# Hybrid attention block on one core: head 0's probabilities of steps 34 to 51 moved by SBUF to SBUF DMAs and turned by VectorE instead of by TensorE

## What is computed

```python
def mixer_b(q, k, v, rel_table):
    ...
    logits = jnp.einsum('bcqhd,bckhd->bhcqk', qc.astype(jnp.float32),
                        kb.astype(jnp.float32)) * SCALE
    ...
    logits = logits + bias[:, None]
    ...
    p = jax.nn.softmax(logits, axis=-1)
    out = jnp.einsum('bhcqk,bckhd->bcqhd', p.astype(vb.dtype), vb)
    return out.reshape(b, s, B_W)
```

## Time and profile before

| what | us |
|---|---|
| median of three runs | 1034.33 (1033.67 to 1035.46) |
| span of the profiled execution | 1031.9 |
| median less the span | 2.4 |
| TensorE busy | 1023.0 |
| VectorE busy | 770.9 |
| ScalarE busy | 470.5 |

### The profile page before, as it was taken

One profiled execution on the slowest core, in us unless ns is written; L12 is line 12 of the kernel. 1 busy time (PEld: TensorE's weight loads), 2 busy tenths in 40 slices (PEclk: granted clock), 3 DMA queues, 4 the chain that ended last, 5 costly groups with the idle time before them and its releaser, 6 DMA issues.

```text
span 1031.9 us, 15795 instructions
## 1 busy us (share of the span) xinstructions
PE 1023.0 (99%) x5525; PEld 851.0 (82%) x5525; DVE 770.9 (75%) x1506; ACT 470.5 (46%) x978; POOL 219.7 (21%) x218
## 2 busy tenths in 40 slices
PE   9999999999999999999999999999999999999997
PEld 8899887788778888878888888888888888888886
DVE  4955677867688578888988788786444777778997
ACT  6632355545477567836221221311344445454562
POOL 5200000000000003148675674761100000000000
PEclk9999999999999999999999999999999999999999
DMA  9835442111071474045444434446777733454344
GB/s 202 222 98 136 108 134 77 42 47 37 11 225 43 123 188 159 21 143 212 171 167 155 163 134 152 163 144 225 243 243 242 229 103 92 143 194 142 93 142 164
DMA packets 135071, 147.92 MB, mean 143 GB/s; under 512 B 72248, under 2 KB 85440, under 8 KB 132944
## 3 DMA queue, kind: packets, MB, share of 16 engines
q1 hardware_dynamic: 133920, 146.68, 45.7%
q10 hardware_dynamic: 688, 0.20, 0.1%
q0 software_dynamic: 384, 0.04, 0.0%
HBM read 103.65 MB, written 47.49 MB: 146 GB/s over the span
## 4 chain that ended last, share of the span: by engine, by line
PE 94%; DVE 3%; issue 1%; DMA 1%; ACT 0%; POOL 0%; DVEq 0%; ACTq 0%; POOLq 0%
PE ps L2242 27%; PE ps L2244 27%; PE ps L2243 27%; PE ps L2451 3%; PE ps L2465 3%; PE ps L2432 2%; PE ps L2376 1%; DVE wc_lo L1918 1%; PE ps L2411 1%; PE ps L2584 1%; PE ps L2586 1%; PE ps L2572 1%; DMA up_raw<-in_w_up 1%; DVE b_lo L1907 1%; PE ps L2254 0%
## 5 line engine op out<-in xcount | busy, mean ns | idle before, releaser
L2242 PE MATMUL ps<-b_hi,wc_hi 128*128 128x512 f32 x448 | 174.6, 390 | 0.5 <-DVE wc_lo L1918 0.5
L2243 PE MATMUL ps<-tm_lo,sm_hi 128*128 128x512 f32 (+1 forms) x450 | 174.6, 388 | 0.0
L2244 PE MATMUL ps<-tm_hi,sm_lo 128*128 128x512 f32 (+1 forms) x450 | 174.6, 388 | 0.0
L2242 PE MATMUL ps<-tm_hi,sm_hi 128*128 128x512 f32 (+1 forms) x450 | 174.6, 388 | 0.0
L2244 PE MATMUL ps<-b_hi,wc_lo 128*128 128x512 f32 x448 | 174.3, 389 | 0.0
L2243 PE MATMUL ps<-b_lo,wc_hi 128*128 128x512 f32 x448 | 174.3, 389 | 0.0
L1485 ACT ACTIVATE sm_hi<-sm_raw 128x512 fp32r<-128x512 f32 x112 | 70.7, 631 | 161.8 <-DMA sm_raw<-u_matrices 161.8
L2146 DVE TENSOR_TENSOR sm_lo<-sm_raw,sm_hi 128x512 fp32r<-128x512 f32 x112 | 77.4, 691 | 77.9 <-ACT sm_hi L1485 77.3
L2242 PEld LDWEIGHTS ps<-b_hi,wc_hi 128*128 128x128 f32 x448 | 84.1, 188 | 18.3 <-DVE wc_lo L1918 0.9
L2242 PEld LDWEIGHTS ps<-tm_hi,sm_hi 128*128 128x128 f32 x450 | 84.5, 188 | 17.6
L2244 PEld LDWEIGHTS ps<-tm_hi,sm_lo 128*128 128x128 f32 x450 | 84.5, 188 | 17.4
(11 more groups left out here) (261 smaller groups left out, 2063.2 us busy)
## 6 DMA issues: line engine op xcount, KB each, us to landing
u_matrices<-stage SPq DMA_DIRECT2D x112, 256.0 KB, 2.0
sm_raw<-u_matrices SPq DMA_DIRECT2D x112, 256.0 KB, 2.6
up_raw<-in_w_up SPq DMA_DIRECT2D x16, 1024.0 KB, 5.0
w<-in_w_down SPq DMA_DIRECT2D x64, 256.0 KB, 3.8
w_raw<-in_w_in SPq DMA_DIRECT2D x8, 512.0 KB, 3.5
xr<-in_x SPq DMA_DIRECT2D x8, 512.0 KB, 4.3
x_rows<-xr SPq DMA_DIRECT2D x8, 512.0 KB, 4.1
xf<-x_rows SPq DMA_DIRECT2D x8, 512.0 KB, 3.5
```

Of the source, the lines that this page charges most:

```text
L2242: pe.matmul(out, w_hi_, x_hi_, start=start, stop=False)
L2243: pe.matmul(out, w_hi_, x_lo_, start=False, stop=False)
L2244: return pe.matmul(out, w_lo_, x_hi_, start=False, stop=stop)
```

## The change

For steps 34 to 51 (`TURNED_B`) head 0 goes another way, as it does in part of group A already. Head 1 stays on TensorE.

- VectorE writes head 0's biased scores back to PSUM. ScalarE's exponential reads them there and writes `prob_b` with the columns regrouped by quarters of 32.
- ScalarE does head 0's scaling (`normalize` on ScalarE), VectorE only its reciprocal.
- Four DMAs, SBUF to SBUF, move the quarters to `turn_in` (one buffer for even, one for odd steps), 128 pieces of 128 bytes times the number of key blocks each. SyncE issues two of them, ScalarE the other two right behind its scaling. They wait for the scaling and for VectorE's turn of step n-2.
- VectorE turns the landed 32 x 32 blocks into `probT_b` (`turn_probs`) one step later, behind its last scaling.
- `weigh` reads head 0's turned blocks in pieces of 32 and writes its PSUM columns with a stride of 4.
- Head 1's chunk stays: one chunk copied by ScalarE, and for five blocks a second of one block copied by VectorE. Bank 5 is not used here any more. In a pair, the second step's chunk is turned after three triples of fill instead of two.
- TensorE waits before `scores(n)` for head 0's exponential of n-1. The values lie in another order, `[P, 10, T, 64]`, which makes room for a buffer. SyncE's weight and bias loads stand between its exchanges.

```diff
-    if paired(n) and nk <= 2:
-        return [(0, 2 * nk, nk == 1)]
+    if turned_b(n):
+        return [(nk, nk, True)] if nk < B_KEYS else [(nk, 4, True), (nk + 4, 1, False)]
...
+TURNED_B = range(A_STEPS + 2, LATE - 2)
...
-        v_tok = sb("v_tok", 64, [P, T, VW])
+        v_tok = sb("v_tok", 64, [P, VW // 64, T, 64])
...
+        turn_in = [sb(f"turn_in{n}", at, [P, B_KEYS * P]) for n, at in enumerate((64, 204))]
...
+        def exchange_quarters(eng, n, quarters):
+
+            m = keys_of(n) * 32
+            eng.wait_ge(s_pb, pb0 + turns_until(n + 1))
+            if n < TURNED_B[2]:
+                eng.wait_ge(s_pv, A_STEPS)
+            else:
+                eng.wait_ge(s_tb, tb0 + turns_until(n - 1))
+            for a in quarters:
+                eng.dma_start(turn_in[n % 2][32 * a:32 * a + 32, 0:4 * m].rearrange("j (c m) -> j c m", c=4),
+                              sent_probs(n)[:, a * m:a * m + m]).then_inc(s_pld[n % 2], 16)
...
-            load_fill(6)
-            load_fill(7)
-            sp.wait_ge(s_nm, 10 * T)
-            load_bias(6)
-            load_fill(8)
-            load_fill(9)
-            sp.wait_ge(s_nm, 12 * T)
-            load_bias(7)
+            for n in range(A_STEPS + 1, LATE):
+                exchange_step(n)
+                if n % T == T - 1:
+                    sp.wait_ge(s_nm, 2 * n + 2)
+                    load_bias(n // T + 2)
+                elif n % 4 == 1 and n // 4 - 2 < FILL_TILES:
+                    load_fill(n // 4 - 2)
...
+            def normalize(n):
+
+                at = 2 * (n % 2)
+                act.wait_ge(s_ri, 2 * n + 1)
+                nc.scalar.activation(sent_probs(n), sent_probs(n), ACT.Copy, scale=rinv[0][:, at:at + 1]).then_inc(s_pb, 1)
...
                         for hh in range(2):
                             exp(m, hh)
+                        if turned_b(m):
+                            normalize(m)
+                            exchange_quarters(act, m, (2, 3))
...
+            def turn_probs(n):
+
+                dve.wait_ge(*exchanged(n))
+                dve.wait_ge(s_pv, n - 1)
+                cols = slice(0, keys_of(n) * P)
+                nc.vector.transpose(prob_t(n, 0)[:, cols], turn_in[n % 2][:, cols]).then_inc(s_tb, 1)
...
+                if turned_b(n - 1):
+                    turn_probs(n - 1)
...
+                    if turned_b(n - 1):
+                        pe.wait_ge(s_exp, 2 * n - 1)
...
+                if turned_b(n):
+                    pe.wait_ge(s_tb, tb0 + turns_until(n + 1))
...
+                        out_ = ps[64 * hh:64 * hh + 64, 7, (t % 4) * P:(t % 4) * P + P]
+                        if hh == 0 and turned_b(n):
+                            out_ = out_.rearrange("p (j c) -> p c j", c=4)
...
-                    if m == first + 2 and n % T == 3:
+                    if m == first + 3 and n % T == 3:
                         transposes(n, 0)
-                        transposes(n, 1)
```

More of the change, by code:

```diff
@@ L224, in chunks_until, with chunk_column @@
     return sum(len(chunks_of(m)) for m in range(n))
+def chunk_column(n, c):
+    if not turned_b(n):
+        return 0
+    return P if n % T == 1 else 0
 def chunk_banks():
@@ L233, in chunk_banks @@
                 bank = (6, 4, 5)[(len(banks) + A_STEPS // 2) % 3]
-            else:
-                bank = 6 if n < A_STEPS else 5 if paired(n) and n % T == 1 else (6, 5, 6)[c]
-            banks[n, c] = bank, last.get(bank)
+            elif turned_b(n):
+                bank = 6
+            else:
+                bank = 6 if n < A_STEPS else (6, 5, 6)[c]
+            banks[n, c] = bank, last.get(bank) if chunk_column(n, c) != P else None
             last[bank] = n, c
@@ L499, in chunk_copy @@
             heads = probT_b[:, 2 * (n % 2):2 * (n % 2) + 2]
-            out = ps[:, CHUNK_BANKS[n, c][0], 0:count * P]
+            at = chunk_column(n, c)
+            out = ps[:, CHUNK_BANKS[n, c][0], at:at + count * P]
+            if turned_b(n):
+                return heads[:, 1, first % nk * P:(first % nk + count) * P], out
             if nk == B_KEYS:
@@ L794, in shift_values @@
                     sp.wait_ge(s_tab, 32 * g)
-                sp.dma_start(v_odd[g][0:64], v_tok[64:P, first - 1:end - 1, 0:P]).then_inc(s_tab, 16)
-                sp.dma_start(v_odd[g][64:P], v_tok[0:64, first:end, 0:P]).then_inc(s_tab, 16)
+                sp.dma_start(v_odd[g][0:64], v_tok[64:P, 0:2, first - 1:end - 1]).then_inc(s_tab, 16)
+                sp.dma_start(v_odd[g][64:P], v_tok[0:64, 0:2, first:end]).then_inc(s_tab, 16)
             shift_values(0)
@@ L2409, in weigh_a @@
                         cols = slice(64 * hh, 64 * hh + 64)
+                        values = odd_values(t)[:, hh] if t and half == 0 else v_tok[:, hh, t]
                         out_ = ps[cols, 7, :].rearrange("p (q i n) -> p q i n", q=2, i=2)[:, (r + 1) % 2, :, 64 * half:64 * half + 64]
-                        last = pe.matmul(out_, values[:, cols], probT_a[r % 2][:, heads, 64 * half:64 * half + 64],
+                        last = pe.matmul(out_, values, probT_a[r % 2][:, heads, 64 * half:64 * half + 64],
                                          start=True, stop=True)
@@ L2447, in transposes @@
                     pe.wait_ge(s_pta if chunks_of(former[0])[former[1]][2] else s_ptd, copied(*former))
-                pe.wait_ge(s_p, 2 * n + (start + count - 1) // nk + 1)
+                pe.wait_ge(s_p, probs_made(n, (start + count - 1) // nk))
                 for i in range(count):
                     hh, k = (start + i) // nk, (start + i) % nk
-                    last = pe.transpose(ps[:, bank, i * P:(i + 1) * P], prob_of(n, hh)[:, c0 + k * P:c0 + (k + 1) * P], ident[:])
+                    at = chunk_column(n, c) + i * P
+                    last = pe.transpose(ps[:, bank, at:at + P], prob_of(n, hh)[:, c0 + k * P:c0 + (k + 1) * P], ident[:])
                 last.then_inc(s_pt, 1)
@@ L2518, in _ @@
                 elif not paired(n - 1):
[L2519 to L2520 removed]
+                    for c in range(1 if turned_b(n - 1) else 2):
+                        transposes(n - 1, c)
                 for m in range(first, end):
[L2522 removed]
+                    if m == first + 3 and n % T == 3:
                         transposes(n, 0)
[L2524 to L2526 removed]
+                    elif m == first + 2 and keys_of(n - 1) == B_KEYS:
+                        transposes(n - 1, len(chunks_of(n - 1)) - 1)
                     fill(m)
```

73 lines of the change are left out of this document (54 added, 19 removed).

## The result

The changed kernel takes **1048.95 us** (median of 4 runs, 1048.25 to 1050.34) beside 1034.0 us (1033.42 to 1035.46) before: a ratio of 1.0147, 95% interval 1.0135 to 1.016. It is slower, as forecast, but by 14.95 us where 4.7 were forecast, and outside the range of 1031 to 1046. The profiled execution took 1048.35 us with a span of 1046.5 us, against 1031.9 before: +14.6 us.

The account below looks back on a forecast made before the run. TensorE, busy for 99% of the span, was taken to bound the kernel. The terms -7.0 + 5.9 + 2.0 + 2.9 + 0.9 = +4.7 us on 1034.33 gave 1039.0 us, range 1031 to 1046.

Parts of the forecast that it names:

- the three kinds of idle time: TensorE idle before 43's turn (some 2 us, three times), before products at 37, 45, 53 (0.65), before a fill.
- term A: Steps 34/35, 42/43, 50/51: TensorE waits for ScalarE's chunk copy behind its DMA issues, 1.95 us three times, +5.9 us.
- d: Time of one DMA issue on ScalarE, taken as 0.63 us; it enters the sum 16 times.
- C and D: Steps 45 to 47, 37 to 39 (+2.9 us) and 39/40, 47/48 (+0.9): TensorE waits for VectorE's late fill eviction.
- B: Steps 36/37, 44/45, 52/53: TensorE waits for VectorE's transpose before the products, 0.65 us three times, +2.0 us.
- Saving: Steps 34 to 51: 67 transposes of head 0 leave TensorE at 0.105 us each, -7.0 us.
- Strided write: Head 0's products with the values write PSUM with a stride: taken as 0, at most 7.8 us.
- Landings, SyncE's issues, value layout: Quarters' landing, SyncE's two issues a step and the values' new first-stage layout: costed at nothing.
- ScalarE's exponential from PSUM: ScalarE reads head 0's scores from PSUM instead of SBUF: 0.12 us shorter for 512 columns.
- rival 1: Issues on ScalarE are cheap (0.05 us, or the engine runs on): -7.0 + 3.8 = -3.2, 1031.1 us; chance 0.14.
- Rival 3: Dearer still: strided write at its bound, 1046.8 us, or queues delaying each other's issues, about 1049 us; chance 0.08.

Follow-up runs that it names:

- The two bank experiments: Against the changed kernel: bank 5 for the second chunk of a pair, 1042.11 us; bank 5 for every second chunk, 1041.74 us.
- the first experiment: The changed kernel with all four quarters of every exchange issued by SyncE and none by ScalarE: 1031.21 us.
- the last: The changed kernel with all quarters issued by SyncE, VectorE's transpose ahead of its scaling at some steps, bank 6 for all chunks: 1029.76 us.
- a bank experiment: The changed kernel with bank 5 instead of 6 for the second chunk of a pair (steps 35, 43, 51): 1042.11 us.

## Why the prediction was wrong

Its sign and its mechanism hold: ScalarE's issues stand in its own stream ahead of a copy that TensorE waits for, and taken away they leave a kernel that is faster than before. The signs that it named are there, 173 transposes of prob_b instead of 240 and the three kinds of idle time. Its size fails in one step, the stop of term A, which was sized too short and priced at its length alone. By the account above, +4.7 was to be -7.0 + 5.9 + 2.0 + 2.9 + 0.9, and +14.6 is -4.8 + 9.5 + 5.1 + 1.0 + 3.0 + 0.8.

- **The step that failed: A, +5.9.** It measured 9.5, and the clock behind its stops took 5.1 more. I had taken d = 0.63 from SyncE's row. SyncE's own issues here have a median of 0.599, but ScalarE's take 0.58 and 0.86 where both queues issue in pairs, and the engine starts its next work 0.1 to 0.4 us after that. The stops were 2.90 to 3.41 us instead of 1.95.
- **The omission inside it: the clock, +5.1.** I priced a stop of TensorE at its length. The earlier trace rows showed 1.00 throughout, in a stage where TensorE never stood, and nothing in that row says what happens when it does.
- **C and D, +3.8.** Right in size, at another instruction. VectorE's lateness was to be met at the eviction, 1.45 us twice and 0.45 twice. It was met at the copy just ahead of it, where the bank rule, which I had read only for the pairs, holds TensorE: 1.26, 1.28, 0.22 and 0.22 us, 3.0 in all. The two bank experiments agree: with that wait taken away it returns at the eviction. Places that I had not walked gave 0.8 more.
- **B, +2.0.** 1.0 in the changed kernel in two waits of 0.43 and 0.57 us, 1.8 in three waits of 0.6 where ScalarE issues nothing or one. The size of each wait, 0.65, was right; at step 37 of the changed kernel TensorE came too late to meet it.
- **Saving, -7.0.** TensorE's busy time fell by 4.8 only, in the first experiment (119.9 to 115.1) and by the account above, and by 6.2 in the last (113.7). The price of 0.105 a transpose stands: six of them took 0.63 us to the next fill before (229.92 to 230.55) and three take 0.30 now (235.23 to 235.53). The lower figure is at least in part waits that busy time hides, such as the 0.22 us at each of the three places of B in the first experiment; I have not traced all of it.
- **Strided write, 0.** Right. The products of two steps with five blocks (40 matmuls in the trace) take 2.33 us to the next instruction in the changed kernel (223.55 to 225.88) as they did before, head 0's written with the stride.
- **Landings, SyncE's issues, value layout, 0.** Issue to landing has a median of 2.3 us. VectorE's transpose waits for them 3.0 us in all in the first experiment, which TensorE sees at most in B. With SyncE's issues doubled no new wait of TensorE comes up.
- **ScalarE's exponential from PSUM** was to be 0.12 us shorter; for 640 columns it is 798 ns against 824 from SBUF, 0.03.

The rivals: rival 1's value for issues that cost nothing, 1031.1, is what the kernel without issues on ScalarE takes (1031.21), by -4.8 + 2.3 and not by -7.0 + 3.8; that the two sums end 0.1 us apart is in part luck. Rival 3 named 1049 us, which is the time by luck, and not the cause: no issue of the changed kernel was doubled to 1.26, the longest took 0.894. *The lock between two sequencers that the Trainium skill's "Perfetto Trace Analysis" (DMA Instruction, HWDGE) describes agrees with the direction in which ScalarE's second issue went, from 0.62 us alone to 0.86 beside SyncE's second. It would not tell why the first, made beside SyncE's first, stays at 0.58; that the lock causes the rise no run shows. The ~50 ns of the Trainium skill's "DMA: Bandwidth & Descriptors" (Anatomy of one DMA) for the gpsimd path bears on none of these issues, as the measured 0.55 us minimum shows.*

## What to carry to other kernels

Price a DMA issue on a computing engine as work of that engine, by the row of that very queue under the same company, and give the issues to the queue on which nothing waits behind them. Price a stop of TensorE at its length and look at the granted clock behind it: each fall cost 1.7 us here on top of the stop. It fell behind all three stops of 2.9 us and more in the change, but also behind one of 1.86 us and not behind another of 1.95, so read the clock from the trace and don't infer it from the length. When one wait of a tight chain is removed, look for the same delay at the next place before counting it as a gain.

## What was unexpected of the hardware

ScalarE's issue of the same descriptors (128 pieces, SBUF to SBUF) took a median of 0.580 us when it issued one beside SyncE's three, and 0.624 when it issued four alone. When both issued two, its first took 0.58 and its second 0.86, while SyncE's stayed at 0.60 wherever it issued. After stops of 2.90 to 3.41 us TensorE's granted clock fell to 0.50 (1.2 GHz) and the mean over the 6.8 to 7.0 us from the stop's end was 0.75; with stops of up to 1.61 us it stayed at 1.00 in the kernel with one issue on ScalarE, but in a bank experiment it fell behind 1.86 us and not behind 1.95. And with 8.6 us of products that compute nothing the kernel was 3.1 us faster by the medians.
